# Grid attention whose keys lie in half column blocks, 256 of them for every query block

## The chip, the cores and the metric

One core of one Trainium2 chip runs the whole program. The metric is the device time of one execution in microseconds, the lower the better. The engines named here are TensorE (PE; its weight loads PEld), VectorE (DVE), ScalarE (ACT), GpSimd (POOL) and SyncE (SP, which issues the DMAs). They run side by side and wait for each other on semaphores.

## The reference, cut to what matters

Two blocks run one after the other in float32 on 512 tokens of width 1024. The first has a gated recurrent layer and an FFN, over the tokens and 16 meta tokens. The second has two attention layers, each followed by an FFN: layer 0 with a window of tokens, layer 1 with a window on a grid. Beside its 12 token heads each layer has 4 memory heads, which attend to 256 memory tokens. Head width is 64. Layer 1, which the change is about:

```python
def neighbourhood_attn(q, k, v, rpb):      # q/k/v (B,S,H,D), S = 512 = 8 rows x 64 columns, H = 12
    rows = S // GRID_W                     # 8, and the window has min(8, rows) = 8 rows: all of them
    ...
    c = jnp.arange(GRID_W)
    col_start = jnp.clip(c - NA_COLS // 2, 0, GRID_W - NA_COLS)          # NA_COLS = 16
    in_win = (c[None, :] >= col_start[:, None]) & (c[None, :] < col_start[:, None] + NA_COLS)
    ...
    bias = rpb.astype(jnp.float32)[:, dr_idx][:, :, :, dc_idx]           # by row and column distance
    s = jnp.einsum('brchd,brijhd->bhrcij', qg, kband).astype(jnp.float32) * (D ** -0.5)
    s = s + bias[None]
    s = jnp.where(in_win[None, None, None, :, None, :], s, NEG_INF)
    p = jax.nn.softmax(s.reshape(sh[:-2] + (kr * GRID_W,)), axis=-1).reshape(sh)
    o = jnp.einsum('bhrcij,brijhd->brchd', p.astype(v.dtype), vband)
```

A query at column c so sees 8 rows x 16 columns of keys: 8 columns to its left, its own and 7 to its right, pushed inwards at the edges.

## The kernel before

**Products.** Weights come by DMA into two slots `raw`, a unit of 128 output columns at a time. Each is split into a rounded part `w_hi` (ACT, `split_hi`, L811) and the rest `w_lo` (DVE, `split_lo`, L1312), and PE makes three products per tile of 128 input features: `z_hi` and `z_lo` with `w_hi` (L2084), `z_hi` with `w_lo` (L2090). PE waits for `lo_done` of a unit. In the recurrent layer's first projection (`gemm("qf", ...)`) a query unit is taken by `outs516` (the last 516 of 528 tokens, two halves of 258) and a forget gate unit by `outs528`; the units of the output gates are read by `out516` too.

**Token order of layer 1.** The 512 tokens are permuted so that 128 neighbouring positions are one column block of the grid: 8 rows x 16 columns. `natural` and `blocked` (L424 to L430) are the two views. The permutation is made when layer 0's last FFN writes its output: ACT writes z in block order (L1044), rounds it (L1046) and squares it (L1049), DVE makes `z_lo` (L1676) and sums the squares; after layer 1's output projection DVE adds the result back through the two views (L1660).

**Projection of queries and keys** (`qk1`): 14 units, 6 of queries, 6 of keys, 2 of memory queries, two heads each. Per unit ACT copies PSUM to `scaled_heads` (L1233, L1235), DVE scales it (L1894), ACT rounds it into `q_pair` or `k_hi` (`rounded_heads`, L1212), DVE subtracts to get the rest (`rest_heads`, L1907). ACT's order is: round unit m-1, round the weights of unit m+2, copy unit m.

**Values** (`v1`): 8 units in two halves, matmuls at L2644. Between those of the second half PE already scores heads 0 and 1.

**Heads.** Query block b (128 queries) has keys in its own block and the neighbouring ones: `span` gives 256, 384, 384 and 256 keys, `key_block` the first block. Per head and block: PE scores with two matmuls (`scores`, L2621 and L2622, keys' high and low part; the queries' two parts lie on top of each other); DVE adds the bias and takes the row maximum (`biased`, L1955, followed by an accumulator read), and after four blocks negates the maxima (L1980; L2038 for memory heads, L1977 in layer 0); ACT takes the exp (`exps`, L1255); PE transposes 128 x 128 pieces (`turn`, L2669), ACT (blocks 0 to 2, L1263) or DVE (block 3, L1972) copies them to SBUF, and PE multiplies with the values (`values`, L2684, two instructions per piece); DVE divides by the sum (L2020, L2022). `step` on each engine is a pipeline over three heads: while head n is scored, head n-1 gets its exps and head n-2 is transposed and multiplied; in PE's order a block's `turn` comes first, then `scores`, then `values` of the block before. ACT's order in a step is copy 0, exp 0, copy 1, exp 1, copy 2, exps 2 and 3, and exp 0 waits for the negated maxima. The memory heads run behind the token heads in the same steps, with 256 keys in every block.

**Bias.** POOL builds a head's bias with three instructions (`biases`, L784): one each for the first, the middle and the last query blocks, from a table slice `rpb_raw` and a mask. Three slots each; bias h waits for its DMA and for the scoring of head h-3 (`ls` at 4h-8). Biases 0 and 1 come once the last queries are split, from bias 2 on POOL waits for the end of the value projection. SP's `bias_load` (L640) issues eight DMAs a head, one per grid row of queries, and waits until bias h-3 is built. In layer 0 the bias is one instruction (L774) from constants, with no DMA.

Of the kernel before, what the change touches and what calls it, by code (L numbers as in the profile page):

```python
# [6 lines left out]
ACT = mybir.ActivationFunctionType  # L7
AX = mybir.AxisListType
F32 = mybir.dt.float32
# [3 lines left out]
P = 128  # L13
D = 1024
KD = D // P
SEQ = 512
# [21 lines left out]
HD = 64  # L38
# [7 lines left out]
BC = GRID_C // 4  # L46
NEG = -1e30
# [29 lines left out]
def build(nc, t):  # L77
# [3 lines left out]
    with ctx:  # L81
# [18 lines left out]
        assert early_con + 4 * GRID_R * (48 + 32 + 32) <= fixed[0]  # L100
# [79 lines left out]
        att_con = sb(at, "att_con", [P, 3 * P + 3 * 48])  # L180
# [5 lines left out]
        rpb_last = sb(at, "rpb_raw2", [P, GRID_R, 48])  # L186
# [14 lines left out]
        first_bias = sb([scratch], "bias0", [P, GRID_R * (48 + 32 + 32)])  # L201
# [3 lines left out]
        rpb_raw = [sb([w_at[i] + 4 * UNIT], f"rpb_raw{i}", [P, GRID_R, 48]) for i in range(2)] + [rpb_last]  # L205
# [3 lines left out]
        last_bias = sb(at, "bias2", [P, GRID_R * (48 + 32 + 32)])  # L209
        bias = [(first_bias, sb([(spare_bias, early_con)[l]], f"bias1_{l}", [P, GRID_R * (48 + 32 + 32)]), last_bias)  # L210
# [291 lines left out]
        def span(memory, b):  # L502

            return (0, NMEM) if memory else ((P, 2 * P), (0, 3 * P), (0, 3 * P), (0, 2 * P))[b]

        def key_block(memory, b, j):

            return j if memory else max(b - 1, 0) + j
# [51 lines left out]
        def _(sp):  # L560
# [118 lines left out]
        def _(pool):  # L679
# [84 lines left out]
            for l in range(2):  # L764
# [5 lines left out]
                def biases(h, g, r):  # L770
# [6 lines left out]
                    else:  # L777
                        pool.wait_ge(rpb_loaded[r], 128 * g + 128)
                        pool.wait_ge(*s.at("ls", 4 * h - 8))
                        at_ = 0  # L780
                        for v, (first, n) in enumerate(((1, 2), (0, 3), (0, 2))):
                            x0 = first * BC
                            mask = att_con[:, 3 * P + 48 * v + x0:3 * P + 48 * v + x0 + n * BC]
                            x = pool.tensor_tensor(  # L784
                                bias[l][r][:, at_:at_ + n * P].rearrange("p (n r c) -> p n r c", n=n, r=GRID_R),
                                rpb_raw[r][:, :, x0:x0 + n * BC].rearrange("p r (n c) -> p n r c", n=n),
                                mask.rearrange("p (n o c) -> p n o c", n=n, o=1)
                                    .to_broadcast([P, n, GRID_R, BC]), ALU.add)
                            at_ += n * P
# [16 lines left out]
        def _(act):  # L806
# [224 lines left out]
            def residual_squares(name, tokens, sems, g=None, g2=None, order=None):  # L1031
# [4 lines left out]
                def one(m, s, width):  # L1036
                    if sems:
                        act.wait_ge(ps_free[s], freed[s] + 2 + m // 2)
                        hi, x, square = z_tile(z_hi, m, tokens), h_tile(tokens, m), sq[s][:, 0:tokens]
                        if order:  # L1040
                            z, x, square = (ur, vr)[s][:, 0:tokens], natural(x), blocked(square)
# [5 lines left out]
                        elif g:  # L1047
                            act.activation(hi, x, ACT.Identity, scale=g(m)).then_inc(sems["z_hi"], 1)
                        act.activation(square, x, ACT.Square).then_inc(sems["sq"], 1)  # L1049
# [148 lines left out]
            def layer(l):  # L1198
# [5 lines left out]
                def rounded_heads(m):  # L1204
# [7 lines left out]
                    act.activation(hi, tile, ACT.Copy).then_inc(s["q_hi"], 1)  # L1212
# [1617 lines left out]
```

## Time and profile before

| what | value |
|---|---|
| timed runs | 2021.03, 2023.68, 2024.14 us; median 2023.68 |
| the profiled execution's own time | 2022.38 us |
| its span in the trace, granted TensorE clock | 2020.4 us, 0.998 |
| PE busy | 1996.0 us (99%), 11631 instructions |
| DVE, ACT, POOL busy | 1086.8 (54%), 863.8 (43%), 189.5 us (9%) |
| chain that ended last, by engine | PE 67%, ACT 1%, DVE 1%, issue 1% |
| DMA | 175.01 MB, mean 87 GB/s |

How to read it: the span is the time between the first and the last instruction; the execution's own time is 2.0 us longer. A busy PE is not yet a PE at its peak, since matmuls overlap each other. The chain follows each instruction back to what released it; its shares of lines and engines leave out what it doesn't name. In the chain a piece lasts until the next begins, so its times add up; in the timeline an instruction's recorded time can overlap its successor's.

### The profile page before, as it was taken

What the parts mean: (1) busy time and instruction counts of PE and PEld (TensorE: products, weight loads), DVE (VectorE), ACT (ScalarE), POOL (GpSimd) and SP (SyncE); (2) the same over time, 40 slices, a digit from 0 to 9 for tenths busy, and PEclk for the clock granted to TensorE, in tenths of its full rate; (3) what the DMA queues carried; (4) which work ended last, traced back from release to release, by engine and by line L of the source; (5) the groups of instructions that cost most, each with busy time, mean ns of one, the idle gap of its engine ahead of it and who ended that gap; (6) DMA issues with size and microseconds to landing.
All of it is one profiled execution on the core that took longest, in us unless ns stands there. A gap on an engine that the chain in (4) does not pass through costs nothing.

```text
span 2020.4 us, 31565 instructions
## 1 busy us (share of the span) xinstructions
PE 1996.0 (99%) x11631; PEld 1754.5 (87%) x11631; DVE 1086.8 (54%) x1864; ACT 863.8 (43%) x1240; POOL 189.5 (9%) x191
## 2 busy tenths in 40 slices
PE   8999999999999999999999999999999999999998
PEld 8989999999988988889988888888889888888887
DVE  4224888556653656577654433444656654434443
ACT  5534555533223454456643322334656543312333
POOL 0004010200100110001001100110014001100100
PEclk9999999999999999999999999999999999999999
DMA  4322111223333233331033332333322133333332
GB/s 139 99 82 84 53 54 53 74 83 94 93 107 107 85 91 114 106 99 37 13 97 98 102 97 83 93 99 89 105 85 66 33 94 93 105 92 91 95 100 77
DMA packets 321921, 175.01 MB, mean 87 GB/s; under 512 B 6560, under 2 KB 319136, under 8 KB 321840
## 3 DMA queue, kind: packets, MB, share of 16 engines
q1 hardware_dynamic: 321840, 173.92, 29.7%
q8 instruction: 51, 0.84, 0.2%
q14 instruction: 30, 0.25, 0.0%
HBM read 171.80 MB, written 2.10 MB: 86 GB/s over the span
## 4 chain that ended last, share of the span: by engine, by line
PE 67%; ACT 1%; DVE 1%; issue 1%; POOL 0%; POOLq 0%; ACTq 0%; DVEq 0%
PE ps L2084 38%; PE ps L2090 19%; PE ps L2684 3%; PE ps L2644 2%; PE ps L2669 2%; PE ps L2621 1%; PE ps L2622 1%; ACT scaled_heads L1233 1%; DVE scaled_heads L1894 1%; PE ps L2563 1%; PE ps L2722 0%; ACT w_hi L811 0%; PE ps L2209 0%; DVE w_lo L1312 0%; PE ps L2468 0%
## 5 line engine op out<-in xcount | busy, mean ns | idle before, releaser
L2084 PE MATMUL ps<-z_hi,w_hi 128*128 128x512 f32 (+2 forms) x2128 | 643.7, 343 | 0.6 <-DVE qf L1425 0.6
L2084 PE MATMUL ps<-z_lo,w_hi 128*128 128x512 f32 (+2 forms) x2128 | 634.6, 339 | 0.0
L1312 DVE TENSOR_TENSOR w_lo<-raw,w_hi 128x1024 fp32r<-128x1024 f32 (+2 forms) x298 | 385.0, 1292 | 433.0 <-ACT w_hi L811 431.5
L811 ACT ACTIVATE w_hi<-raw 128x1024 fp32r<-128x1024 f32 (+2 forms) x298 | 328.2, 1101 | 440.4 <-PE ps L2090 403.9
L2090 PE MATMUL ps<-z_hi,w_lo 128*128 128x512 f32 (+2 forms) x2128 | 445.8, 339 | 0.0
L2084 PEld LDWEIGHTS ps<-z_hi,w_hi 128*128 128x128 f32 x2128 | 367.4, 189 | 51.0 <-issue 4.1
L2084 PEld LDWEIGHTS ps<-z_lo,w_hi 128*128 128x128 f32 x2128 | 366.1, 189 | 44.7
L2090 PEld LDWEIGHTS ps<-z_hi,w_lo 128*128 128x128 f32 x2128 | 345.6, 189 | 45.0
L2084 PE MATMUL ps<-g_hi,w_hi 128*128 128x512 f32 (+1 forms) x539 | 209.7, 390 | 0.5 <-POOL g_lo L739 0.5
L2084 PE MATMUL ps<-g_lo,w_hi 128*128 128x512 f32 (+1 forms) x539 | 208.9, 389 | 0.0
L739 POOL TENSOR_TENSOR g_lo<-gv,g_hi 128x512 f32 x66 | 85.7, 1299 | 1064.2 <-ACT g_hi L1178 1064.2
L2090 PE MATMUL ps<-g_hi,w_lo 128*128 128x512 f32 (+1 forms) x539 | 145.8, 388 | 0.0
L1660 DVE TENSOR_TENSOR H<-H,ps 128x512 f32<-128x512 f32 (+2 forms) x56 | 38.6, 689 | 164.5 <-PE ps L2090 164.5
L2084 PEld LDWEIGHTS ps<-g_hi,w_hi 128*128 128x128 f32 x539 | 101.4, 188 | 23.5 <-POOL g_lo L739 1.9
L2084 PEld LDWEIGHTS ps<-g_lo,w_hi 128*128 128x128 f32 x539 | 101.4, 188 | 21.6
L1178 ACT ACTIVATE g_hi<-gv 128x512 f32 (+1 forms) x66 | 41.7, 632 | 181.1 <-DVE gv L1857 181.1
L2090 PEld LDWEIGHTS ps<-g_hi,w_lo 128*128 128x128 f32 x539 | 99.9, 188 | 21.7
L2084 PE MATMUL ps<-mix_hi,w_hi 128*128 128x258 f32 (+1 forms) x256 | 76.3, 339 | 0.0
L2084 PE MATMUL ps<-mix_lo,w_hi 128*128 128x258 f32 (+1 forms) x256 | 76.1, 338 | 0.0
L1255 ACT ACTIVATE ls<-ls,neg_max 128x256 f32<-128x256 f32 (+1 forms) x128 | 65.5, 540 | 1.6 <-DVE neg_max L1980 1.6
L2684 PEld LDWEIGHTS ps<-v_tok,pts 128*128 128x128 f32 x480 | 63.7, 191 | 0.9 <-ACT v_tok L1248 0.4
L2684 PE MATMUL ps<-v_tok,pts 128*128 128x65 f32 x480 | 64.2, 265 | 0.1
(330 smaller groups left out, 2317.6 us busy)
## 6 DMA issues: line engine op xcount, KB each, us to landing
raw<-w_gate_up SPq DMA_DIRECT2D x88, 512.0 KB, 3.9
raw<-w_down SPq DMA_DIRECT2D x48, 704.0 KB, 4.6
raw<-w_in SPq DMA_DIRECT2D x44, 512.0 KB, 3.9
raw<-w_up SPq DMA_DIRECT2D x44, 512.0 KB, 3.9
raw<-w_out SPq DMA_DIRECT2D x24, 512.0 KB, 3.7
raw<-w_in_b SPq DMA_DIRECT2D x14, 512.0 KB, 3.9
raw<-w_in_a SPq DMA_DIRECT2D x12, 512.0 KB, 3.7
raw<-w_branch SPq DMA_DIRECT2D x8, 512.0 KB, 3.7
```

The source lines that it names most:

```text
L739: pool.tensor_tensor(lo, src, hi.bitcast(F32), ALU.subtract).then_inc(done, 1)
L811: act.activation(w_hi[s][:, 0:width], raw[s][:, 0:width], ACT.Copy).then_inc(hi_done, 1)
L1178: act.activation(g_hi[:, j, 0:tokens], gv[:, 0:tokens], ACT.Copy).then_inc(s["hi"], 1)
L1233: x = act.activation(scaled_heads[half][rows, j:j + 1, :], heads, ACT.Copy)
L1255: act.activation(ls(r, b)[:, lo:lo + width], ls(r, b)[:, lo:lo + width], ACT.Exp, bias=neg_max[r][:, b:b + 1])\
L1312: dve.tensor_tensor(w_lo[s][:, 0:width], raw[s][:, 0:width], w_hi[s][:, 0:width].bitcast(F32), ALU.subtract).then_inc(lo_done, 1)
L1660: dve.tensor_tensor(tile, tile, more, ALU.add).then_inc(ps_free[s], 1)
L2084: pe.matmul(out, w_hi[s][:, w0 + k * P:w0 + (k + 1) * P], rhs[:, lo:lo + width], start=a, stop=False)
L2090: x = pe.matmul(out, w_lo[s][:, w0 + k * P:w0 + (k + 1) * P], rhs_hi[:, lo:lo + width], start=False, stop=last)
L2644: x = pe.matmul(v_bank(l, half, c)[:, 0:width], zz[:, k, c * P:(c + 1) * P], ww[i % 2][:, kk_ * width:(kk_ + 1) * width], start=a, stop=b)
L2669: x = pe.transpose(ps[3][:, b % 2, j * P:(j + 1) * P], ls(r, b)[:, lo + j * P:lo + (j + 1) * P], ident)
L2684: x = pe.matmul(y_bank(r)[:, b * VS:(b + 1) * VS], pts[b % 2][:, j * P:(j + 1) * P], v, start=j == 0, stop=j == width // P - 1)
```

## The change

Half column blocks: `blocked` and `natural` now work on 8 half blocks of 8 rows x 8 columns (64 positions each). The keys and values are kept in an order turned by one half block: the last half block first, then 0 to 6. Query block b stays 16 columns wide (half blocks 2b and 2b+1); its keys are then the turned positions from 128 b on, 256 of them, and for b = 3 they wrap round to the first 128. z is written in the turned order by two ACT instructions, and so are its squares; queries are turned back when they are rounded and subtracted, in two pieces (`TURNED`). The bias table is laid out on the host as a full 128 x 256 per head, one DMA each; POOL's three instructions are all 256 wide, in runs of 8. The diff, cut to its core (sizes of buffers and the added argument `l` of `span` are left out):

```diff
 BC = GRID_C // 4
+HB = BC // 2
...
         def natural(x):
-            return x.rearrange("p (r b c) -> p b r c", r=GRID_R, b=4)
+            return x.rearrange("p (r b c) -> p b r c", r=GRID_R, c=HB)
         def blocked(x):
-            return x.rearrange("p (b r c) -> p b r c", r=GRID_R, b=4)
+            return x.rearrange("p (b r c) -> p b r c", r=GRID_R, c=HB)
+        TURNED = ((slice(0, 7 * HD), slice(HD, SEQ)), (slice(7 * HD, SEQ), slice(0, HD)))
+        def turned_blocks(x):
+            return ((blocked(x)[:, 1:], slice(0, 7)), (blocked(x)[:, 0:1], slice(7, 8)))
...
+        def span(memory, b, l):
+            return (0, NMEM) if memory or l else ((P, 2 * P), (0, 3 * P), (0, 3 * P), (0, 2 * P))[b]
+        def key_block(memory, b, j, l):
+            if memory:
+                return j
+            return (b + j) % 4 if l else max(b - 1, 0) + j
...
             def bias_load(h, r):
                 sp.wait_ge(*atts[1].at("bias", h - 2))
-                for rq in range(GRID_R):
-                    rows = slice(GRID_R - 1 - rq, 2 * GRID_R - 1 - rq)
-                    sp.dma_start(rpb_raw[r][rq * BC:(rq + 1) * BC, :, :],
-                                 t["rpb"][bass.ds(h, 1), :, rows, :].rearrange("o c r x -> (o c) r x"))\
-                      .then_inc(rpb_loaded[r], 16)
+                sp.dma_start(rpb_raw[r][:, :], t["rpb"][bass.ds(h, 1), :, :].rearrange("o q x -> (o q) x"))\
+                  .then_inc(rpb_loaded[r], 16)
...
-                        for v, (first, n) in enumerate(((1, 2), (0, 3), (0, 2))):
-                            x0 = first * BC
-                            mask = att_con[:, 3 * P + 48 * v + x0:3 * P + 48 * v + x0 + n * BC]
+                        for v in range(3):
+                            mask = att_con[:, 3 * P + 4 * HB * v:3 * P + 4 * HB * (v + 1)]
                             x = pool.tensor_tensor(
-                                bias[l][r][:, at_:at_ + n * P].rearrange("p (n r c) -> p n r c", n=n, r=GRID_R),
-                                rpb_raw[r][:, :, x0:x0 + n * BC].rearrange("p r (n c) -> p n r c", n=n),
-                                mask.rearrange("p (n o c) -> p n o c", n=n, o=1)
-                                    .to_broadcast([P, n, GRID_R, BC]), ALU.add)
+                                blocked(bias[l][r][:, v * NMEM:(v + 1) * NMEM]), blocked(rpb_raw[r][:, :]),
+                                mask.rearrange("p (n o c) -> p n o c", o=1, c=HB).to_broadcast([P, 4, GRID_R, HB]),
+                                ALU.add)
...
-                            act.activation(blocked(z), x, ACT.Identity, scale=g(m)).then_inc(sems["z"], 1)
+                            for to, blocks in turned_blocks(z):
+                                done = act.activation(to, x[:, blocks], ACT.Identity, scale=g(m))
+                            done.then_inc(sems["z"], 1)
                             act.wait_ge(*sems.at("z", m + 1))
                             act.activation(hi, z, ACT.Copy).then_inc(sems["z_hi"], 1)
+                            for to, blocks in turned_blocks(square):
+                                done = act.activation(to, x[:, blocks], ACT.Square)
+                            done.then_inc(sems["sq"], 1)
...
-                    act.activation(hi, tile, ACT.Copy).then_inc(s["q_hi"], 1)
+                    if l and (m < queries or m >= queries + keys):
+                        for to, of in TURNED:
+                            done = act.activation(hi[:, :, to], tile[:, :, of], ACT.Copy)
+                    else:
+                        done = act.activation(hi, tile, ACT.Copy)
+                    done.then_inc(s["q_hi"], 1)
...
-                    dve.tensor_tensor(lo, tile, hi.bitcast(F32), ALU.subtract).then_inc(s["q_lo"], 1)
+                    if l and (m < first_key or m >= first_key + keys):
+                        for to, of in TURNED:
+                            done = dve.tensor_tensor(lo[:, :, to], tile[:, :, of], hi[:, :, to].bitcast(F32), ALU.subtract)
+                    else:
+                        done = dve.tensor_tensor(lo, tile, hi.bitcast(F32), ALU.subtract)
+                    done.then_inc(s["q_lo"], 1)
...
-                    pe.matmul(bank, q_pair[:, n_, b * P:(b + 1) * P], hi[:, head, lo:lo + width], start=True, stop=False)
-                    pe.matmul(bank, q_pair[:, n_, b * P:(b + 1) * P], rest_[:, head, lo:lo + width],
-                              start=False, stop=True).then_inc(s["s"], 1)
+                    if l and not memory and b == 3:
+                        bank = chunked(bank, 2)
+                        hi, rest_ = (chunked(x[:, head, :], 4)[:, ::-3] for x in (hi, rest_))
+                    else:
+                        hi, rest_ = (x[:, head, lo:lo + width] for x in (hi, rest_))
+                    pe.matmul(bank, q_pair[:, n_, b * P:(b + 1) * P], hi, start=True, stop=False)
+                    pe.matmul(bank, q_pair[:, n_, b * P:(b + 1) * P], rest_, start=False, stop=True).then_inc(s["s"], 1)
```

## Rows read from the trace of the kernel before

**Rows 1.** Stretches: us, engines' busy us and counts, PE clock, DMA share, GB/s
```profile
1526.00:1577.00 51.00, 50.88 (x449) 50.32 (x448) 36.81 (x153) 38.16 (x86) 23.76 (x30) 1.00 0.19 42
```

**Rows 2.** The chain, one grid token head: start, us, what
```profile
1541.53 0.33 PE ps L2669 x3
1541.86 0.18 PE ps L2621
...
1542.22 0.62 PE ps L2684 x6
1542.83 0.23 PE ps L2669 x2
...
1544.38 0.39 PE ps L2684 x4
...
1545.84 0.33 PE ps L2669 x3
```

**Rows 3.** The chain again, one memory head
```profile
1578.43 0.39 PE ps L2684 x4
...
1581.85 0.39 PE ps L2684 x4
```

**Rows 4.** First attention layer's timeline: start, us, engine, line, instruction
```profile
951.06 0.89 DVE L1977 SCALAR_TENSOR_TENSOR neg_max<-row_max,par,minus 128x4 f32<-128x4 f32 x1
...
951.11 0.83 POOL L774 TENSOR_TENSOR bias<-att_con,con 128x384 f32<-128x384 f32 x1 [3.50 <-DVE row_max L1955]
```

**Rows 5.** Timeline, a memory head's step in the grid layer
```profile
1581.82 0.16 DVE L2038 SCALAR_TENSOR_TENSOR neg_max<-row_max 128x4 f32<-128x4 f32 x1
...
1582.02 0.51 ACT L1255 ACTIVATE ls<-ls,neg_max 128x256 f32<-128x256 f32 x1
...
1582.50 0.38 ACT L1263 ACTIVATE pts<-ps 128x256 f32<-128x256 f32 x1
...
1583.39 0.55 PE L2684 MATMUL ps<-mv,pts 128*128 128x65 f32 x4
```

**Rows 6.** Waits in the grid layer's head stage: us, times, longest
```profile
POOL bias L784 <- DMA rpb_raw<-rpb: 13.7, 7, 3.0
```

**Rows 7.** DMA issues: count, KB each, median us to landing
```profile
rpb_raw<-rpb SPq DMA_DIRECT2D x96, 24.0 KB, 1.7
```

**Rows 8.** Groups, grid then first layer: count | busy us, mean ns | idle
```profile
L784 POOL TENSOR_TENSOR bias<-rpb_raw,att_con 128x256 f32<-128x256 f32 x20 | 14.6, 732 | 40.9 <-PE ps L2644 27.2 <-DMA rpb_raw<-rpb 13.7
...
L784 POOL TENSOR_TENSOR bias<-rpb_raw,att_con 128x384 f32<-128x384 f32 x10 | 10.1, 1006 | 0.0
...
L774 POOL TENSOR_TENSOR bias<-att_con,con 128x384 f32<-128x384 f32 x10 | 8.2, 826 | 34.4 <-DVE row_max L1955 23.0 <-PE ps L2644 11.4
```

**Rows 9.** Timeline of POOL, the start of bias 2
```profile
1526.33 0.74 POOL L784 TENSOR_TENSOR bias<-rpb_raw,att_con 128x256 f32<-128x256 f32 x1 [27.22 <-PE ps L2644]
```

**Rows 10.** Waits of DVE in the grid layer's head stage
```profile
DVE pts L1972 <- PE ps L2622: 6.8, 14, 0.6
```

**Rows 11.** Timeline at the end of the query and key projection
```profile
1488.51 1.06 ACT L1212 ACTIVATE q_pair<-scaled_heads 64x1024 fp32r<-64x1024 f32 x1 [1.33 <-DVE scaled_heads L1894]
...
1492.70 1.76 DVE L1312 TENSOR_TENSOR w_lo<-raw,w_hi 128x768 fp32r<-128x768 f32 x1
...
1494.51 0.80 PE L2644 MATMUL ps<-w_hi,z_hi 128*128 128x384 f32 x3 [1.01 <-DVE w_lo L1312]
```

**Rows 12.** Timeline, a query unit of the same projection
```profile
1450.70 1.06 ACT L811 ACTIVATE w_hi<-raw 128x1024 fp32r<-128x1024 f32 x1 [0.90 <-PE ps L2090]
```

**Rows 13.** Before that projection: DVE's timeline, then the chain
```profile
1412.31 0.69 DVE L1676 TENSOR_TENSOR z_lo<-cv,z_hi 128x512 fp32r<-128x512 f32 x1 [1.53 <-ACT z_hi L1046]
...
1415.61 0.79 PE ps L2199 x8
```

**Rows 14.** Timeline, residual of the grid layer's output projection
```profile
1640.50 0.69 DVE L1660 TENSOR_TENSOR H<-H,ps 128x512 f32<-128x512 f32 x1 [1.35 <-PE ps L2090]
```

**Rows 15.** Groups by shape in the recurrent layer's first projection
```profile
L2084 PE MATMUL ps<-z_hi,w_hi 128*128 128x258 f32 x122 | 24.7, 284 | 0.6 <-DVE qf L1425 0.6
```

More of the change, by code:

```diff
@@ L99, in build @@
         all_masks = sb(fixed, "masks", [P, LEVELS * P + CONV - SEQ], U8)
-        assert early_con + 4 * GRID_R * (48 + 32 + 32) <= fixed[0]
+        assert early_con + 4 * 3 * NMEM <= fixed[0]
         lbc = sb(fixed, "lbc", [P, 5, KD])
@@ L204, in build @@
         ls_second = [sb([tails[b]], f"ls1_{b}", [P, 3 * P]) for b in range(4)]
-        rpb_raw = [sb([w_at[i] + 4 * UNIT], f"rpb_raw{i}", [P, GRID_R, 48]) for i in range(2)] + [rpb_last]
+        rpb_raw = [sb([w_at[i] + 4 * UNIT], f"rpb_raw{i}", [P, NMEM]) for i in range(2)] + [rpb_last]
         assert at[0] <= scratch
@@ L1253, in exps @@
                     for b in blocks:
-                        lo, width = span(memory, b)
+                        lo, width = span(memory, b, l)
                         act.activation(ls(r, b)[:, lo:lo + width], ls(r, b)[:, lo:lo + width], ACT.Exp,
@@ L1259, in copy @@
                 def copy(h, memory, b):
-                    _, width = span(memory, b)
+                    _, width = span(memory, b, l)
                     act.wait_ge(*s.at("t", 4 * h + (b + 1)))
@@ L1968, in copy @@
                 def copy(h, memory, b):
-                    _, width = span(memory, b)
+                    _, width = span(memory, b, l)
                     dve.wait_ge(*s.at("t", 4 * h + (b + 1)))
@@ L2662, in turn @@
                 def turn(h, r, memory, b):
-                    _, width = span(memory, b)
-                    lo = span(memory, b)[0]
+                    _, width = span(memory, b, l)
+                    lo = span(memory, b, l)[0]
                     pe.wait_ge(*s.at("exp", 4 * h + (b + 1)))
@@ L2673, in values @@
                 def values(h, r, memory, b, kv, n_):
-                    _, width = span(memory, b)
+                    _, width = span(memory, b, l)
                     if b == 0:
@@ L2678, in values @@
                     for j in range(width // P):
-                        block = key_block(memory, b, j)
+                        block = key_block(memory, b, j, l)
                         if memory:
@@ L2763, in attention_constants @@
     import numpy as np
-    a = np.zeros((P, 3 * P + 3 * 48), np.float32)
+    a = np.zeros((P, 3 * P + 3 * 4 * HB), np.float32)
     distance = np.abs(np.arange(P)[:, None] + P - np.arange(3 * P)[None, :])
     a[:, 0:3 * P] = np.where(distance <= P, distance, -1e3 * NEG)
-    x = np.arange(48)[None, :]
+    x, q = np.arange(4 * HB)[None, :], np.arange(P)[:, None]
     for v, b in enumerate((0, 1, 3)):
-        column = BC * b + np.arange(P)[:, None] % BC
+        column = BC * b + q // HD * HB + q % HB
         start = np.clip(column - BC // 2, 0, GRID_C - BC)
-        key = BC * (b - 1) + x
-        a[:, 3 * P + 48 * v:3 * P + 48 * (v + 1)] = np.where((key >= start) & (key < start + BC), 0, NEG)
+        key = BC * b - HB + x
+        a[:, 3 * P + 4 * HB * v:3 * P + 4 * HB * (v + 1)] = np.where((key >= start) & (key < start + BC), 0, NEG)
     return a
@@ L2808, in laid_out @@
         out[k] = a[k]
-    padded = np.pad(a["rpb_b_2"][0], ((0, 0), (0, 0), (BC, BC + 1)))
-    out["rpb"] = np.stack([padded[:, :, BC - 1 - c:4 * BC - 1 - c] for c in range(BC)], axis=1)
+    q, key = np.arange(P)[:, None], np.arange(NMEM)[None, :]
+    down = key // HB % GRID_R - q // HB % GRID_R + GRID_R - 1
+    across = key // HD * HB - HB + key % HB - (q // HD * HB + q % HB) + BC - 1
+    out["rpb"] = a["rpb_b_2"][0][:, down, np.clip(across, 0, 2 * BC - 2)]
     out["attention_constants"] = attention_constants()
```

35 lines of the change are left out of this document (15 added, 20 removed).

## The prediction

> **What bounds the kernel now.** The page comes first: TensorE (PE) is busy 99% of the span and the chain that ended last is mostly PE, so only time taken off PE, or a wait put in its way, can move the end. Then the busy times around the grid attention (the second attention layer): from 1526 to 1577 us PE is busy 50.9 of 51.0 us at a granted clock of 1.00, the upper level, while DVE has 36.8 and ACT 38.2 us of work [rows 1]. Then the chain in that stretch, one pattern per head and all of it PE: for each query block transposes, two score matmuls, and the value matmuls of the block before. One head takes 1541.53 to 1545.84 = 4.31 us [rows 2]. Last the memory heads behind it, whose four blocks are already 256 keys wide: 1578.43 to 1581.85 = 3.42 us per head, still without a PE gap [rows 3].
>
> **What the narrower blocks remove.** The token heads of this layer have 256+384+384+256 = 1280 keys over the four query blocks; the change gives 4 x 256 = 1024. Each head sheds two 128-key pieces, and its period should go to the memory heads' 3.42: 0.89 us less. The parts:
> - transposes: three take 0.33, two 0.23 [rows 2], 0.11 less (a piece is 0.33 / 3) in each of two blocks, 0.22 a head;
> - values: three pieces are six instructions in 0.62, two are four in 0.39 [rows 2], 2 x 0.23 = 0.45 a head;
> - scores: the rest, 0.22 for four matmuls, which agrees with 0.18 for a 384-wide one [rows 2], by its columns 0.12 for a 256-wide one.
>
> All twelve heads pay it on PE (the first two heads' scores lie between the value projection's matmuls, where PE is not idle either): 12 x 0.89 = 10.7 us. The wrapped fourth block (keys read as piece 3, then piece 0) has no row; I take the jump between whole pieces as free, as the row it is nearest to (the plain 256-wide one). At worst its 24 matmuls cost a 384-wide one each, 24 x 0.06 = 1.4 us; a gain is excluded, since its columns are the same.
>
> **What the shorter step runs into.** The place that matters is the small DVE instruction that negates the row maxima (L1980). GpSimd (POOL) may build the bias of head h once head h-3 is scored, the very moment at which DVE starts that negation. In the first attention layer, where no DMA stands between, POOL starts at 951.11 for 0.83 and the negation, begun at 951.06, takes 0.89 us [rows 4]; where nothing meets it takes 0.16 [rows 5]. So it waits out one POOL instruction. In the grid layer POOL still waits for its bias DMAs, 13.7 us over 7 times [rows 6], 96 transfers or 8 a head [rows 7], and that moves most meetings apart. With one transfer a head I expect that wait to go and the meeting to become regular. The Trainium skill, SBUF — State Buffer, section "Who interferes with whom", says that a DVE instruction with two SBUF inputs and a GpSimd one that reads SBUF lock each other out for a whole instruction, the first to issue winning. The trace agrees on the block and its length; on who wins it does not, since the negation's record begins 0.05 us earlier and it still waits.
>
> A POOL instruction now takes 0.732 us for 256 elements in 16 runs of 16, 1.006 for 384 in 24 runs, and 0.826 for 384 in one run in the first layer [rows 8]. The last two put a run at 0.18 / 24 = 7.5 ns; 256 elements in 32 runs of 8 then take 0.73 + 16 x 0.0075 = 0.85 us. Bounds: 0.73 (runs are free) and 1.01 (the 384-wide row).
>
> What a negation of N = 0.06 + 0.85 = 0.91 us does to PE, in the memory heads' pattern [rows 5]: it starts at 1581.82; the exp starts 0.04 after its end; the next copy 0.40 later (an exp takes 0.50, 0.1 of it beside what follows), takes 0.38, and about 0.1 for the hand-over. PE wants the copy for the second value group at 1583.39. So PE waits 1582.74 + N - 1583.39 = N - 0.65 = 0.26 us; the bounds give 0.14 and 0.42. Seven negations (heads 2 to 8) can meet biases 5 to 11. But biases 2 to 4 can start only at 1526.33 [rows 9], behind the value projection, and keep POOL behind for some heads more: there the negation meets a random point of an instruction and costs PE about nothing. I take four heads, 1.0 us; bounds 4 x 0.14 = 0.6 and 7 x 0.42 = 2.9. The first step of the stage loses 0.1 more for the same reason.
>
> DVE itself has 51.0 - 36.8 = 14.2 us free over twelve steps, 1.2 a head [rows 1]; half a microsecond of it a head stands before its copy of the fourth block [rows 10]. It must give up 0.89, gets 0.26 back (two 384-wide instructions become 256-wide), and pays up to 0.45 more for the negation: 1.08 of 1.2. It fits, barely; that is a rival.
>
> **What the turned order adds.** Queries go to their place by two ACT copies and two DVE subtractions, not one, in 8 units. The second ACT instruction costs its fixed part: an exp of 256 occupies 0.40, a rounding of 1024 lasts 1.06 [rows 5, 11], so 0.66 for 768 elements and 0.40 - 0.22 = 0.18 fixed. In the six query units ACT waits 0.90 us for PE ahead of each weight rounding [rows 12]; that covers it, and DVE's second piece too. At the end of the projection nothing does: the rounding of the first memory queries (1488.51) leads through ACT and DVE to the weight subtraction at 1492.70, for which PE idles 1.01 us [rows 11]. So 0.18 goes straight to the end, and as POOL's first biases meet DVE in the same microseconds (that subtraction took 1.76 us) it may be 0 or 0.6. I take 0.3.
>
> The normalisation ahead writes z and its squares in two pieces each, 0.4 us more on ACT per tile. Only the last tile could show: its low part runs from 1412.31 to 1413.0, and the last products that need it end where the sums start, at 1415.6, so they begin at about 1414.9: 1.9 us of cover against 0.4, and 1.5 for the squares' sum behind it [rows 13]. Nothing; with the cover gone it would be 0.4 once. The output projection's residual on DVE reads runs of 8 in place of 16: 0.69 us with runs now, and it waited 1.35 for PE [rows 14]; nothing. SP issues 84 DMAs fewer and stands in no one's way now: PE waits for no weight transfer in this layer.
>
> **The half named first.** The diff holds nothing of the recurrent layer: the kernel before already takes its queries as 2 x 258 = 516 tokens [rows 15], and the gates likewise in the code. I count 0.
>
> **Sum.** 10.7 - 1.0 - 0.1 - 0.3 = 9.3 us. The profiled execution took 2022.4 us: 2013.1. The median of the timed runs is 1.3 us above it: 2014.4. I say 2014.0 us.
>
> **Rivals.**
> - *DVE becomes the bound.* For: 1.08 of 1.2 us used, and in-order waits rarely pack that well. Against: the memory heads keep PE's pace with nearly the same DVE work. If nine heads cost 0.35 more each, 3 us go back: 2017.
> - *Little is left:* hand-overs, wrapped block and query rounding all at their bad ends (2.9 + 1.4 + 0.6) and DVE's 3 us on top of them: 10.7 - 7.9 = 2.8, 2020 to 2021.
> - *POOL sets the pace, slower.* Biases 2 to 11 are 30 POOL instructions from 1526.3, and head 11 is scored only behind them; its step now starts nine steps after the stage's begin, some 9 x 4.31 + 0.3 = 39.1 us later, at 1565.5. At 1.6 us an instruction that is 48 us against 39.2, less 2.6 gained elsewhere: 6 us slower, 2028. It decides from about 1.4 us, that is 40 ns a run in place of 7.5. The Trainium skill, GPSIMD Engine Reference, section 7 "Performance pitfalls for Q7 kernels", names such a price: about 102 cycles for each small read command. By that (an estimate) 24 runs as commands would add some 2 us to an instruction that takes 1.006, so the trace speaks against it.
> - *The change does not do what it says:* true for its first half, and counted.
>
> **Chances and range.** Forecast 0.71; DVE bound 0.17; little left 0.07; POOL's pace 0.05. What a measurement can tell from no change is 0.2%, 4 us: faster 0.88, same 0.07, slower 0.05. Range: the fastest run before less 10.7 is 2010.3; the upper end lies past the DVE case, 2018.
>
> **What would show it.** Right: a period of 3.4 to 3.7 us per token head in the chain; L784 in one form of 256, 36 times, at 0.8 to 0.9 us; POOL waiting for DVE's row maxima and not for DMA; the negation near 0.9 us for about four heads; PE waits of 0.1 to 0.3 on ACT's copies; PE's idle time behind the query rounding 0.3 longer. Wrong: a period of 4 or more with DVE in the chain, POOL instructions above 1.2 us, or fourth-block score matmuls longer than the others.

## The result, and the profile after

The changed kernel takes 2011.7 us (median of five runs, 2009.77 to 2014.73) against 2022.34 us for the kernel before beside it (2020.87 to 2024.14): ratio 0.9948, 95% interval 0.9933 to 0.9962. That is 10.6 us faster; the forecast was 2014.0 us, with a range of 2010.3 to 2018. The profiled execution of the changed kernel is the longest of its five, 2014.73 us, with a span of 2012.9 us, and reaches the changed part 3.2 us later than the profile of before does, for a reason that is not the change's (last section). So stages are compared here, not whole spans. "The stage" runs from ACT's first copy of scales in the projection of queries and keys of the grid layer to PE's first transpose behind the last head. Both kernels have 428.0 us left behind it. It begins with this row in the timeline of before, and with the next one in that of after (start, us, engine, line, instruction, idle time and releaser):

```profile
1420.21 0.60 ACT L868 ACTIVATE sig<-ps 128x512 f32<-128x512 f32 x1 [2.42 <-PE ps L2209]
```

```profile
1423.43 0.60 ACT L870 ACTIVATE sig<-ps 128x512 f32<-128x512 f32 x1 [2.43 <-PE ps L2227]
```

and the whole stage, before and then after (us, each engine's busy us and count, granted clock, DMA share, GB/s):

```profile
1420.21:1592.43 172.22, 169.88 (x1076) 155.40 (x1075) 111.17 (x260) 111.11 (x194) 31.91 (x36) 1.00 0.27 73
```

```profile
1423.43:1584.93 161.50, 159.03 (x1005) 144.84 (x1003) 106.64 (x268) 107.30 (x202) 28.43 (x36) 1.00 0.26 73
```

172.22 - 161.50 = 10.72 us, all of it work taken off PE, whose busy time falls by 169.88 - 159.03 = 10.85, at the upper clock level in both. Beside [rows 1], the same 51 us hold more instructions of the heads on PE, DVE and ACT, and PE is idle for 0.35 us in all:

```profile
1526.00:1577.00 51.00, 50.65 (x463) 50.48 (x462) 39.55 (x185) 42.15 (x105) 20.91 (x30) 1.00 0.10 30
```

The chain of one token head, to be laid beside [rows 2]: 1540.57 to 1543.99 is 3.42 us: transposes, two scores and values, four times over, and every piece is PE's.

```profile
1540.57 0.22 PE ps L2691 x2
1540.80 0.12 PE ps L2644
1540.91 0.12 PE ps L2645
1541.03 0.39 PE ps L2706 x4
...
1543.99 0.22 PE ps L2691 x2
```

Groups of that stretch by shape (count, busy us, mean ns): the token heads' scores cost what the memory heads' do. The wrapped fourth block is one in four of the first group and has no row of its own.

```profile
L2644 PE MATMUL ps<-k_hi,q_pair 128*128 128x256 f32 x42 | 15.2, 361 | 0.0
...
L2644 PE MATMUL ps<-mk_hi,q_pair 128*128 128x256 f32 x16 | 5.8, 364 | 0.0
```

POOL against [rows 6 to 8]: one form of 256 instead of three, one DMA a head, and the wait is for DVE's row maxima. The group (of the whole execution), the wait and the DMA:

```profile
L788 POOL TENSOR_TENSOR bias<-rpb_raw,att_con 128x256 f32<-128x256 f32 x36 | 28.4, 825 | 168.6 <-DVE q_pair L1922 135.3 <-PE ps L2666 27.1 <-DVE row_max L1973 6.1
```

```profile
POOL bias L788 <- DVE row_max L1973: 6.1, 5, 1.3
```

```profile
rpb_raw<-rpb SPq DMA_DIRECT2D x12, 128.0 KB, 2.5
```

The group's mean of 825 ns is not the price of an instruction. The first six, at the end of the query projection, take 7.53 us beside DVE's work, 1.25 each; the 30 between 1526 and 1577 us take 20.91, 0.70 each.

The timeline shows the meeting of POOL and the negation. First POOL's backlog of fifteen instructions, during which three negations take 0.63, 0.61 and 0.62 us; then the regular pattern, beside [rows 4]:

```profile
1529.01 10.37 POOL L788 TENSOR_TENSOR bias<-rpb_raw,att_con 128x256 f32<-128x256 f32 x15 [27.14 <-PE ps L2666]
...
1529.82 0.63 DVE L1998 SCALAR_TENSOR_TENSOR neg_max<-row_max 128x4 f32<-128x4 f32 x1
...
1546.99 0.16 DVE L1998 SCALAR_TENSOR_TENSOR neg_max<-row_max 128x4 f32<-128x4 f32 x1
1547.10 2.10 POOL L788 TENSOR_TENSOR bias<-rpb_raw,att_con 128x256 f32<-128x256 f32 x3 [1.31 <-DVE row_max L1973]
```

The last row is three instructions in 2.10 us: 0.70 each where POOL runs freely. All negations behind those three take 0.16.

### The profile page after: what moved, and what is told of

Same layout as the page of the kernel before. It is cut to its first block, busy times and chain, and to the rows that moved or that the text cites. A ratio compares the mean times of both kernels' runs of the same rounds, so it can differ in the third digit from the quotient of the medians.

```text
span 2012.9 us, 31243 instructions
## 1 busy us (share of the span) xinstructions
PE 1988.2 (99%) x11559; PEld 1745.6 (87%) x11559; DVE 1082.1 (54%) x1872; ACT 862.3 (43%) x1264; POOL 186.1 (9%) x191
## 4 chain that ended last, share of the span: by engine, by line
PE 67%; ACT 1%; DVE 1%; issue 1%; POOL 0%; POOLq 0%; ACTq 0%; DVEq 0%
PE ps L2102 39%; PE ps L2108 19%; PE ps L2706 3%; PE ps L2666 2%; PE ps L2691 2%; PE ps L2644 1%; PE ps L2645 1%; ACT scaled_heads L1246 1%; PE ps L2581 1%; DVE scaled_heads L1907 1%; PE ps L2744 0%; ACT w_hi L813 0%; PE ps L2227 0%; DVE w_lo L1325 0%; PE ps L2486 0%
## 5 line engine op out<-in xcount | busy, mean ns | idle before, releaser
L1183 ACT ACTIVATE sig<-cv 128x512 f32<-128x512 f32 x44 | 27.8, 632 | 81.1 <-DVE cv L1857 81.1
L2706 PE MATMUL ps<-v_tok,pts 128*128 128x65 f32 x432 | 58.8, 263 | 0.4 <-ACT pts L1276 0.4
```

The costliest lines, as they stand in the source:

```text
L1183: act.activation(sig[:, 0:tokens], ur[:, 0:tokens], ACT.Sigmoid).then_inc(s["sig"], 1)
L2706: x = pe.matmul(y_bank(r)[:, b * VS:(b + 1) * VS], pts[b % 2][:, j * P:(j + 1) * P], v, start=j == 0, stop=j == width // P - 1)
```

## The experiments

Stage times are from one profile each. Times are medians (four to ten executions, but one alone in experiments 5 to 8), and ratios are against the kernel before in the same session.

**1. One DMA a head in the kernel before, its widths kept.**

```diff
-                for rq in range(GRID_R):
-                    rows = slice(GRID_R - 1 - rq, 2 * GRID_R - 1 - rq)
-                    sp.dma_start(rpb_raw[r][rq * BC:(rq + 1) * BC, :, :], ...)
+                sp.dma_start(rpb_raw[r][:, :, :], t["rpb"][bass.ds(h, 1), :, :, :].rearrange("o q r x -> (o q) r x"))
```

> The kernel before with the bias table of a head in one DMA (192 KB, laid out on the host) instead of eight; blocks as before. Measure: the stage from ACT's copy of the token scale at the start of the query projection to the first transposes of the output, 172.2 us before and 161.5 us after. Theory 1 (the narrow blocks carry the whole gain, DMA issues were hidden behind a 4.31 us head): stage 172.2 +- 0.3 and the same time within 0.2%. Rival (part of the gain was SP's issue time or late biases): stage shorter by 1 us or more. Side question: POOL should now wait for DVE's row maxima and not for DMA, and the negation should take 0.16 us where it starts 0.1 us ahead of POOL, 0.7 or more if POOL wins.

Measured: 2023.63 us, ratio 1.0002 (0.9992 to 1.0011), stage 172.25 against 172.22. POOL no longer waits for a DMA, only for row maxima, and the negations are 0.16 behind the third. The DMA alone brings nothing.

**2. The changed kernel with eight DMAs a head.**

```diff
-                sp.dma_start(rpb_raw[r][:, :], ...)
+                for rq in range(GRID_R):
+                    rows = slice(rq * BC, (rq + 1) * BC)
+                    sp.dma_start(rpb_raw[r][rows, :], t["rpb"][bass.ds(h, 1), rows, :].rearrange("o q x -> (o q) x"))
```

> The changed kernel with each head's table fetched in eight DMAs of 16 KB again. SP needs about 0.51 us per issue (18 issues in 9.26 us before), 4.1 us a head, more than the 3.42 us that a head now takes. Theory 1: SP sets the pace; the bias of head 11 comes at about 1563.6 us of the changed kernel's clock where the head could start at 1560.2, so the stage grows from 161.5 by about 3.4 us to 165, POOL waits for DMA and DVE for POOL. Rival (the three bias slots hide it): stage 161.5 +- 0.3.

Measured: 2015.99 us, ratio 0.9966 (0.9955 to 0.9977), stage 165.48: 3.98 longer than in the changed kernel. Its waits in the head stage (us, times, longest) show the way: the transfers hold POOL, POOL the biased scores, and these PE's transposes. Of the 4.0 us, 1.8 are such waits; PE's busy time is 161.12 us in place of 159.03, so the rest lies in longer records of its matmuls.

```profile
POOL bias L790 <- DMA rpb_raw<-rpb: 11.8, 6, 3.3
...
DVE ls L1975 <- POOL bias L790: 6.7, 5, 2.8
```

```profile
PE ps L2693 <- DVE row_max L1975: 1.8, 3, 1.4
```

What holds the transfers is SP, which issues nine heads' DMAs in one row, its pauses included: 39.91 / 9 = 4.4 us a head, more than 3.42, and the 16 KB of one land in a median of 1.7 us.

```profile
1517.52 39.91 SPq L649 DMA_DIRECT2D rpb_raw<-rpb  x72
```

With heads of 3.42 us the single DMA is a necessary part: without it 4.0 of 10.7 us are lost, though by itself (experiment 1) it earns nothing.

**3. The changed kernel with the old widths** (2, 3, 3 and 2 blocks of 128 keys).

```diff
-            return (0, NMEM) if memory or l else ((P, 2 * P), (0, 3 * P), (0, 3 * P), (0, 2 * P))[b]
+            if l and not memory:
+                return 0, (2 * P, 3 * P, 3 * P, 2 * P)[b]
+            return (0, NMEM) if memory else ((P, 2 * P), (0, 3 * P), (0, 3 * P), (0, 2 * P))[b]
```

> The changed kernel with the second and third query block of each grid head 384 keys wide again in scores, bias, exps, transposes, copies and values (the third piece is a wrong one, so the attention's result is not the reference's); order of tokens, split queries, bias layout and one DMA a head stay. Theory 1: everything that the change moves is the width, so the stage goes back by 12 x 0.89 = 10.7 us to 172.2 +- 0.4 and the time is that of the kernel before within 0.2%. Rival (the turned order, split copies or POOL's runs of 8 cost or gain something): stage off 172.2 by 1 us or more.

Measured: 2022.07 us, ratio 0.9996 (0.9986 to 1.0006), stage 171.87. The chain shows the old pieces back, a middle block and the next one's end:

```profile
1537.69 0.33 PE ps L2693 x3
...
1539.45 0.61 PE ps L2708 x6
```

So at the old width the turned order, the two-piece roundings, the runs of 8 and the DMA together are worth 0.35 us of the stage; the width is the other 10.4. At the new width the single DMA alone is worth 4.0 (experiment 2): the parts do not simply add up.

**4. POOL's first biases wait for one unit more of the queries.**

```diff
-                pool.wait_ge(*s.at("q_lo", (9, 13)[l]))
+                pool.wait_ge(*s.at("q_lo", (9, 14)[l]))
```

> The changed kernel, but POOL waits for the last query unit's split (the 14th in place of the 13th) before bias 0, so it no longer works beside the weight subtraction for which PE idles 0.9 us at the start of the value projection. Theory 1 (POOL and DVE block each other there, 1.49 us in place of 0.95): PE idles 0.4 us, stage 161.0. Rival (ACT's copies alone set that moment): PE idles 0.9 us as now, stage 161.5. A time difference of 0.5 us is below what can be told, so the trace decides.

Measured: 2011.09 us, ratio 0.9944 (0.9927 to 0.9961), stage 160.93, 0.57 less than the changed kernel. PE's idle time ahead of the second value unit (timeline; the bracket is the idle time), changed kernel and this one:

```profile
1497.62 0.97 PE L2666 MATMUL ps<-w_hi,z_hi 128*128 128x384 f32 x4 [0.89 <-DVE w_lo L1325]
```

```profile
1493.77 0.97 PE L2666 MATMUL ps<-w_hi,z_hi 128*128 128x384 f32 x4 [0.30 <-DVE w_lo L1325]
```

The weight subtraction just ahead takes 1.49 us beside POOL and 0.94 without it. The meeting with POOL was 0.59 of that wait of 0.89.

**5. The negation 0.1 us later** by two one-column memsets ahead of it.

```diff
+                        dve.memset(late_pair[0][:, :], 0.0)
+                        dve.memset(late_pair[1][:, :], 0.0)
                         dve.scalar_tensor_tensor(neg_max, ...)
```

> The changed kernel with two one-column memsets (0.06 us each) on DVE ahead of the negation of the row maxima in the grid layer. In the changed kernel the negation starts 0.11 us ahead of POOL's bias and takes 0.16 us, so the stall that was forecast did not come. Theory 1 (who starts first decides): the negation now starts after POOL and waits for its whole instruction, 0.6 to 0.75 us for heads 5 to 8; it ends some 0.8 us after the last row maximum, so by the forecast's formula PE waits 0.1 to 0.2 us at the second value group, and such a head takes 3.5 to 3.6 us in place of 3.42; stage 162.0 to 162.5 in place of 161.5. Rival A (POOL never blocks this instruction in this layer): 0.16 us as before. Rival B (blocked, but PE has slack): 0.7 us and 3.42 a head.

Measured: 2011.70 us, stage 161.59. The edit didn't do what it was for: two memsets in a row record 0.06 us each but shift the negation by little, and it starts 0.10 ahead of POOL as before and takes 0.16.

```profile
1547.28 0.16 DVE L2001 SCALAR_TENSOR_TENSOR neg_max<-row_max 128x4 f32<-128x4 f32 x1
...
1547.38 2.12 POOL L789 TENSOR_TENSOR bias<-rpb_raw,att_con 128x256 f32<-128x256 f32 x3 [1.31 <-DVE row_max L1974]
```

It tests neither theory; experiment 7 takes its place.

**6. POOL builds every bias twice** (the price of a POOL instruction doubled).

```diff
-                        for v in range(3):
+                        for i, v in enumerate((0, 1, 2, 0, 1, 2)):
+                            if i == 3:
+                                x.then_inc(extra, 1)
+                                pool.wait_ge(extra, h + 1)
```

> The changed kernel with every bias of the grid layer built twice (six POOL instructions a head, same result), the second set behind a semaphore of the first. An instruction takes 0.70 us back to back, so a head needs 4.2 to 4.4 us of POOL. Theory 1 (POOL sets the pace as in the slower rival of the prediction): biases 2 to 11 take 60 x 0.7 = 42 us or a little more from the end of the value projection where head 11 could start after 31.3, so the stage grows by 11 to 13 us, to 172.5 to 174.5; DVE waits for POOL. Rival (slots and slack hide it): under 5 us more.

Measured: 2021.59 us, stage 171.42, 9.9 longer than in the changed kernel. POOL is the chain, six instructions a head, 4.25 us from head to head; between 1540 and 1580 us DVE waits 10.4 us for biases:

```profile
1549.40 4.17 POOL bias L792 x6
```

```profile
DVE ls L1977 <- POOL bias L792: 10.4, 7, 1.5
```

The rival in which POOL sets the pace is a real mechanism. In the changed kernel it is about 1.0 us a head away from deciding: ten biases have some 9 x 3.42 + 0.3 = 31.1 us, 3.1 each, and three instructions of 0.70 take 2.1. PE's clock stands at 1.2 GHz for 3.4 us of this run's stage (1532 to 1536 us), while the chain is POOL's.

**7. Starts swapped at the meeting.** DVE clears 256 columns ahead of the grid layer's negation, POOL clears one column ahead of the first layer's bias.

```diff
+                        if h >= 3:                          # first layer, POOL
+                            pool.memset(late_cell[:, :], 0.0).then_inc(extra, 1)
+                            pool.wait_ge(extra, h - 2)
...
+                        dve.memset(late_tile[:, :], 0.0)    # grid layer, DVE
```

> The changed kernel with the two starts exchanged: in the grid layer DVE writes a 256-column memset ahead of the negation, so that POOL's bias starts first; in the first attention layer POOL writes one column and waits for itself ahead of its bias, so that the negation starts first. Two one-column memsets were too little: the negation still started 0.09 us ahead of POOL and took 0.16. Theory 1 (who starts first by more than about 0.05 us holds the other off): in the grid layer the negation of heads 5 to 8 takes 0.5 to 0.7 us and ends 0.80 to 0.85 us after the old start; by the forecast's formula PE then waits 0.15 to 0.2 us a head, period 3.6, stage 0.8 to 1.4 us longer than 161.5. In the first layer it takes 0.22 us in place of 0.89 and nothing moves, since PE waits for neither. Rival A: durations stay (the kind of instruction decides, not the order). Rival B: they swap, but the period stays 3.42 (the formula is wrong).

Measured: 2012.23 us, stage 163.67 (+2.17). In the first layer the negation falls from 0.89 to 0.22. POOL's large instruction now begins 0.21 us behind it in place of 0.05; the negation's record was the first in both.

```profile
958.08 0.22 DVE L2001 SCALAR_TENSOR_TENSOR neg_max<-row_max,par,minus 128x4 f32<-128x4 f32 x1
...
958.11 0.10 POOL L784 MEMSET late_cell<- 128x1 f32 x1 [3.30 <-DVE row_max L1979]
...
958.29 0.83 POOL L786 TENSOR_TENSOR bias<-att_con,con 128x384 f32<-128x384 f32 x1
```

The grid layer's half missed. POOL starts 0.02 us behind the memset and 0.16 ahead of the negation, and the negation still takes only 0.10. Perhaps the memset holds the place for it; no run shows why. But one head met POOL's backlog. The chain shows the whole path of a late negation to PE, and the timeline its record:

```profile
1532.11 0.25 DVE late_tile L2004
1532.36 2.28 DVE neg_max L2005
...
1535.07 0.37 ACT pts L1282
...
1535.49 0.66 PE ps L2713 x4
```

```profile
1532.27 2.35 DVE L2005 SCALAR_TENSOR_TENSOR neg_max<-row_max 128x4 f32<-128x4 f32 x1
```

PE waited 1.8 us there. The forecast's formula, N - 0.65 with N = 0.25 + 2.28 = 2.53, gives 1.9. The other 0.4 of the 2.17 is in no wait of PE that the view shows.

**8. Queries rounded in one piece.**

```diff
-                    if l and (m < queries or m >= queries + keys):
-                        for to, of in TURNED:
-                            done = act.activation(hi[:, :, to], tile[:, :, of], ACT.Copy)
+                    done = act.activation(hi, tile, ACT.Copy)
```

(and the same for DVE's subtraction)

> The changed kernel with queries rounded and subtracted in one instruction each again (queries are then not turned back, so the attention's result is not the reference's). Theory 1: the split costs 0.1 us of ACT and 0.1 of DVE per unit, covered but for the last two; PE starts the value projection's second unit up to 0.2 us earlier after the scale copy than the 74.2 us of the changed kernel. Rival (the meeting of POOL's first biases with DVE decides that moment): it starts between 0.3 earlier and 0.6 later, as in the kernel before, 74.3.

Measured: 2014.6 us, beside the 2014.73 of the changed kernel's profiled execution, whose stretches at the lower clock are the same; stage 161.36 against 161.50. PE's idle time is 0.74 instead of 0.89 and its second value unit comes 74.03 instead of 74.19 us behind the stage's begin, 0.16 less. The two roundings, of one piece and of two, show where 0.09 of it is from; the subtraction adds the other 0.07 (1.22 and 1.29):

```profile
1491.72 1.06 ACT L1220 ACTIVATE q_pair<-scaled_heads 64x1024 fp32r<-64x1024 f32 x1 [1.33 <-DVE scaled_heads L1903]
```

```profile
1491.72 1.15 ACT L1222 ACTIVATE q_pair<-scaled_heads 64x896 fp32r<-64x896 f32 x2 [1.33 <-DVE scaled_heads L1907]
```

**9. Weights rounded ahead of the queries, in both layers** (with the late biases of 4).

```diff
-                    if m:
-                        rounded_heads(m - 1)
                     ...                      # the weights of unit m + 2
+                    if m:
+                        rounded_heads(m - 1)
```

> The changed kernel with POOL's first biases one unit later and, in both query and key projections, ACT rounding the next weights (and DVE subtracting them) ahead of the heads of the unit before, not after. In the key units ACT's copies, DVE's scaling, ACT's rounding and ACT's weight rounding follow each other in 5.73 us a unit where PE needs 5.53; with the weights first, the weight rounding lies beside DVE's scaling and the loop is 2.40 + 1.23 + 1.06 = 4.7 us. Theory 1: PE is no longer late at the value projection (idle 0.89 us in the changed kernel, 0.30 with the late biases), stage 160.5 to 160.9, about 0.8 us below the changed kernel's 161.5, which the time alone can hardly show. Rival (another wait takes its place, the first head's rounding now being later): stage 161.5 or more.

Measured: 2013.96 us, ratio 0.9957 (0.9943 to 0.997), stage 161.89, 0.4 longer. It missed twice: in the grid layer DVE's last weight subtraction still stood behind its scaling of unit 13, and in the first layer the heads' queries came too late, which costs another 2.0 us ahead of the stage. PE's waits between 700 and 1500 us:

```profile
PE ps L2644 <- DVE q_pair L1924: 2.0, 1, 2.0
PE ps L2666 <- DVE w_lo L1325: 0.9, 1, 0.9
```

**10. The same in the grid layer alone, with DVE's subtraction moved as well.**

```diff
-                    if m:
+                    if m and l == 0:
                         rounded_heads(m - 1)
                     ...                      # the weights of unit m + 2
+                    if m and l:
+                        rounded_heads(m - 1)
```

> The changed kernel with three moves about the query rounding, the computation unchanged. In the grid layer alone ACT and DVE round each unit's weights ahead of the heads of the unit before (after_weights_first had this in both layers, and TensorE waited 2.0 us for query heads in the first one); DVE's subtraction of the last unit's weights stands ahead of its scaling of unit 13's heads; POOL's first biases of the grid layer wait for unit 14's rounding, as in after_bias_late. Theory (the wait in front of TensorE's second value unit, 0.89 us in the changed kernel, is one chain: the rounding of the first memory queries, the weights' rounding, DVE's weight subtraction behind its work on the heads of unit 13, slowed by POOL): with the weights ahead of all of that the wait goes to 0 to 0.1 us, the stage from the scale copy to the first mix transposes takes 160.3 to 160.7 us in place of 161.50, and the time is 0.9 us below the changed kernel's median at the same number of half-clock stretches: 2010 to 2011.5. Rival: the wait only moves, to the first heads' scores, whose queries are now rounded later (query parts, TensorE idle at the first score matmuls): then the stage stays at 161.0 or above and the time at the changed kernel's.

Measured: 2010.94 us (2010.66 to 2014.46), ratio 0.9946 (0.9933 to 0.996). PE waits for nothing at the second value unit, but the stage takes 160.73, 0.2 less than with late biases alone and 0.77 less than the changed kernel, not 0.89 and more: behind the last query unit the chain now goes through the rounding of queries (1.13) and ACT's copy, and PE takes over from these.

```profile
1491.83 1.13 ACT q_pair L1222 x2
...
1493.59 0.60 ACT scaled_heads L1250
...
1494.23 1.85 PE ps L2670 x9
```

It has the shortest stage of all. The ratios of the changed kernel, of experiment 4 and of this one have intervals that overlap; that this one is faster than the changed kernel is read from the stage, not shown by the times.

## Why the prediction was right, step by step

- **Narrower blocks, 10.7 us: right.** A head takes 3.42 us, as its memory heads did [rows 3], and experiment 3 gives 10.4 for the width. From the second value unit to the end of the heads the kernels differ by 97.92 - 87.31 = 10.61 us; 12 x 0.89 = 10.68. The wrapped block is free: a head that holds one takes what a memory head takes, and the group's mean is 361 ns against 364.
- **Negation against POOL, 1.0 us: mis-sized, it is 0.1.** Two things were wrong. POOL's instruction takes 0.70, not 0.85: runs of 8 cost nothing over runs of 16, the lower bound. The 384-wide row of the first layer [rows 8], from which the run's price was taken, has other operands, so that price was not one of runs. (The group's 825 ns lies in the forecast's "0.8 to 0.9" by luck: it is the first six that raise it.) And I took a meeting 0.05 us apart [rows 4] to stand for this one. Here the negation starts 0.11 us ahead of POOL and is through in 0.16. The kernel before had such a meeting in the grid layer itself, with POOL 0.10 us behind:

```profile
1539.82 0.16 DVE L1980 SCALAR_TENSOR_TENSOR neg_max<-row_max 128x4 f32<-128x4 f32 x1
...
1539.92 0.73 POOL L784 TENSOR_TENSOR bias<-rpb_raw,att_con 128x256 f32<-128x256 f32 x1 [2.99 <-DMA rpb_raw<-rpb]
```

  In the first layer experiment 7 turns 0.89 into 0.22 by moving POOL's start alone. What is left in the changed kernel is three heads in the backlog, each 3.45 in place of 3.42, which no run takes apart further. The formula N - 0.65 fits where it could be tried (0.63 gives below zero; 2.53 gives 1.9, measured 1.8). It has the copy 0.40 us behind the exp, where [rows 5] show 0.48; experiment 7's late copy came 0.41 behind. That four meetings would be aligned was a guess on a lead of some hundredths of a microsecond, which [rows 4] could not settle.
- **The first step, 0.1 more: not told apart.** The second value unit to the end of the heads gained 10.61 where the widths alone give 10.68. That leaves 0.07 for this and the three heads together.
- **Query rounding, 0.3: right mechanism, half the size, and then covered.** ACT's second instruction costs 0.09, not 0.18, DVE's 0.07; together 0.16, which is what experiment 8 gives. Against that the weight subtraction beside POOL took 1.49 instead of 1.76 [rows 11], and the net is 74.30 - 74.19 = 0.11 gained, where 0.3 lost was forecast; PE's idle time there is 0.89 and not the 1.3 that was named as a sign. That POOL's first biases stretch it was named, with bounds 0 to 0.6; experiment 4 puts it at 0.59.
- **DMA wait: right that it goes.** I gave it no value of its own and used it to align meetings. Experiment 2 shows what it does: 4.0 us, not through the negation but because eight issues a head take SP longer than a head of 3.42 us, and POOL waits for them. In the kernel before, heads of 4.31 and the three slots hid it (experiment 1). The forecast did not see this; its sum took no harm, since the change has the single DMA.
- **DVE the bound: didn't come.** DVE is busy for 39.55 of the 51 us, and from 1531 to 1577 us no piece of the chain is its.
- **Sum.** 10.72 measured against 9.3; the 1.4 between are the negation (0.9), the query rounding (0.3 + 0.1) and the first step. From the median before, 2022.34 - 10.7 = 2011.6, and 2011.7 is measured. The forecast of 2014.0 stands 2.3 us above that: 1.4 by these terms, and 0.9 because it starts from 2014.0 + 9.3 = 2023.3, near the 2023.68 of the first three runs.
- **Counted at 0: right.** The recurrent layer is untouched, and the stage's end leaves both kernels 428.0 us, the residual with its runs of 8 included. z in two pieces costs ACT 0.91 in place of 0.73 us, and its squares 0.70 in place of 0.61. Yet from the last z to the stage it is 9.4 us in both, and what differs ahead of it is the clock (below).

## To carry over

Where the chain is one engine's own instructions, count them and take their durations from a neighbour that already has the new shape: that gave 10.68 of 10.72 us. A transfer pattern that the old pace hides has to be priced at the new pace. Do not count on or fear a collision that hangs on less than 0.1 us; carry it as a bound, and look first for a meeting of the same two instructions in the layer that is changed.

## What the hardware showed beside that

**Who waits, DVE or POOL.** In the first layer the negation's record begins 0.05 us ahead of POOL's, and it takes 0.89 us; so in [rows 4] and in the changed kernel (timeline):

```profile
954.30 0.89 DVE L1995 SCALAR_TENSOR_TENSOR neg_max<-row_max,par,minus 128x4 f32<-128x4 f32 x1
...
954.35 0.83 POOL L780 TENSOR_TENSOR bias<-att_con,con 128x384 f32<-128x384 f32 x1 [3.50 <-DVE row_max L1973]
```

In the grid layer the order of the two records decides. A lead of 0.09 to 0.11 us gives 0.16. So does a lead of 0.01, in experiment 6 (timeline, then the chain), while 0.01 behind POOL the negation of the kernel before waits (timeline):

```profile
1532.37 0.16 DVE L2002 SCALAR_TENSOR_TENSOR neg_max<-row_max 128x4 f32<-128x4 f32 x1
```

```profile
1532.38 4.19 POOL bias L792 x6
```

```profile
1561.39 0.73 POOL L784 TENSOR_TENSOR bias<-rpb_raw,att_con 128x256 f32<-128x256 f32 x1 [1.77 <-DMA rpb_raw<-rpb]
```

```profile
1561.40 0.73 DVE L1980 SCALAR_TENSOR_TENSOR neg_max<-row_max 128x4 f32<-128x4 f32 x1
```

So no lead in the records is a threshold for both layers; why the first layer's instruction, which has other operands, loses with 0.05 is open. Among POOL instructions that follow each other without a gap, the changed kernel's three negations waited only for the rest of one (0.61 to 0.63 us). That of experiment 7 waited for the rest of one and three more (2.35 us). The Trainium skill, SBUF — State Buffer, section "Who interferes with whom", has the first to issue win for one instruction. The grid layer's meetings here agree with that; the first layer's 0.05, the negation behind a memset (experiment 7) and the 2.35 us do not.

**Stretches at the lower clock, ahead of the change.** The changed kernel's profiled run reaches the stage 3.2 us later than that of before. The time arises near 330 and 857 us, in code that the change leaves alone. The granted clock of two windows tells why (before, after, and the kernel of experiment 2; the third column from the end is the clock; the second window is shown for the changed kernel, and is at 1.00 in the other two):

```profile
331.00:338.00 7.00, 7.00 (x48) 7.00 (x48) 6.03 (x19) 3.65 (x7) 0.00 (x0) 0.77 0.01 2
```

```profile
331.00:338.00 7.00, 7.00 (x36) 7.00 (x35) 5.76 (x17) 3.46 (x6) 0.00 (x0) 0.54 0.01 2
856.00:861.00 5.00, 5.00 (x32) 5.00 (x32) 3.47 (x15) 1.39 (x4) 0.00 (x0) 0.66 0.34 100
```

```profile
331.00:338.00 7.00, 7.00 (x62) 7.00 (x61) 6.42 (x21) 4.05 (x7) 0.00 (x0) 1.00 0.01 2
```

Just ahead of the first window PE has little to do in all three (0.51 to 0.69 of 2 us); in the changed kernel:

```profile
328.00:330.00 2.00, 0.69 (x6) 0.48 (x4) 1.45 (x3) 2.00 (x5) 0.00 (x0) 1.00 0.79 234
```

In the first window the clock stands at 1.2 GHz for 6.8 us in the changed kernel's run, for 3.4 in that of before and not at all in the third; in the second window for 3.4 us in the changed kernel's run alone. The stage begins at 1423.4, 1420.2 and 1418.7 us. Over the profiles of this study the begin goes with the time spent at 1.2 GHz: none 1418.6 to 1418.7, 3.4 us 1420.2 to 1420.4, 6.8 us 1421.6 to 1422.1, 10.2 us 1423.4. So each 3.4 us cost some 1.6. (The profile of experiment 9 has 3.4 us and begins at 1422.25: the rest is the 2.0 us that PE waits there in the first layer.) The timed runs of the changed kernel lie in steps of about that size (2009.77, 2010.0, 2011.7, 2013.12, 2014.73), and their mean granted clock falls from 0.998 to 0.996 along them. That this is the whole of their scatter is likely, not shown. What decides in an execution whether the clock falls there was not tried.
